# Tiles at new addresses, later rotary angles, and attention latents scaled after their projections

## The chip, the cores and the metric

One NeuronCore of one Trainium2 chip runs the whole program in one launch. The metric is the device time in microseconds (us), as the median of repeated executions; an execution that is profiled also gives a trace with a start and a duration for each instruction.

## The reference, cut to what matters

Two blocks of two layers each work on 256 tokens of width 1024. The first has a gated mixer, a banded attention and two gated feed-forward parts with a short convolution; the second has a hybrid mixer, latent attention (MLA), two feed-forward parts and two gated per-layer embeddings. Everything is float32. The change touches the MLA and the feed-forward part before it:

```python
c = hn @ w_down                       # 384 query latents, 256 key/value latents, 32 rotary
q = (rmsnorm_2(cq, q_norm) @ w_uq).reshape(b, s, MLA_HEADS, MLA_NOPE + MLA_ROPE)
kv = (rmsnorm_2(ckv, kv_norm) @ w_ukv).reshape(b, s, MLA_HEADS, MLA_NOPE + MLA_V)
q = concat([q_nope, apply_rope(q_rope, positions)]); k = concat([k_nope, rope(kr)])
o = causal_softmax_attention(q, k, v, 1 / sqrt(96));  return o.reshape(...) @ w_o
```

`rmsnorm_2` divides each token's row by its root mean square and multiplies by a gain per feature. Both `@` after it are linear, so a token's root may be put on before or after them.

## The kernel before, in words

Activations lie transposed, 128 features in the partitions and 256 tokens along the free axis: `hT` is the residual, `xt` scratch, and `xA`, `xB`, `hid` hold an activation split in a high and a low float32r part. Weights stream from HBM in 203 chunks of 128 x 2048 float32 (1 MB). SyncE loads them into four buffers `raw0..3`, ScalarE rounds each chunk to `w_hi` (`split_hi`, line 504), VectorE makes the rest `w_lo` (`split_lo`, line 1104), and TensorE multiplies: every 128 x 128 block of weights is used in three products, high by high, high by low, low by high.

There are two forms of these products. In the wide form (`three`, lines 1845 to 1847, and `plain`, line 1856, at the start of a stage) the weights are the stationary operand and the activation, 256 tokens of it, is the moving one. In the natural form (`three_natural`, lines 1851 to 1853) it is the other way round: the activation is stationary and 256 (for the MLA's values 512) columns of weights move.

The order is written out by hand on each engine, in program order, with semaphores between engines. `hi_made`, `lo_made` and `chunk_used` count chunks: `split_hi` of a chunk waits until the chunk four before it has been used, and each stage calls the two splits with `.ahead()`, which is three chunks on.

The last feed-forward part before the MLA has 11 chunks in its second half ("down"). When its last gated pair is written (`hid_lo`), GpSimd issues two DMAs, the MLA's constants `ml_con` and the positions `ml_pos` (lines 483, 484). VectorE then waits for both, computes the rotary angles (`rope_angles`, lines 1132 to 1149, ten chained instructions on 128 x 256), and only then starts on the down loop's splits; ScalarE has the sine of the angles (line 613) before its own splits.

In the MLA, `latent` (line 998) copies the down-projection's result to `ml_c`, squares it into `xt`, and rounds the key/value latents into `xA[3:5]`. TensorE sums the squares over the features (`latent_sums`), ScalarE and VectorE make the inverse root (`inverse_root`, `refine`), VectorE scales the latents by gain and root (`scale_latent`), and ScalarE and VectorE split them again (`round_latent`, `rest_latent`). The keys are already computed from latents without their root and scaled when they are read out of PSUM (`k_scale`); the values and the queries use latents with it. Eight products for the keys go to PSUM banks `K_BANK`, the four for the values to `V_BANK`, and the queries' to banks 0 and 1 in turn; a bank's new product waits until its old content has been read out.

Of the kernel before, what the change touches and what calls it, by code (L numbers as in the profile page):

```python
# [27 lines left out]
P = 128  # L28
T = 256
# [60 lines left out]
K_BANK, V_BANK, O_BANK = (0, 1, 2, 3, 7, 0, 1, 2), (3, 7, 0, 1), (0, 1, 6, 7)  # L90
# [37 lines left out]
def build(nc, stream, x_t, vecs, wst, bsp, rel, hyc, w0, lora, mlc, pos, p_t, out):  # L128
    with ExitStack() as ctx:
# [19 lines left out]
        with ExitStack() as ph:  # L149
# [29 lines left out]
            with ExitStack() as f:  # L179
                ml_q = sb("ml_q", [P, KD, T], where=f)  # L180
                ml_rope_q = sb("ml_rope_q", [P, KD, T], where=f)
                ml_k = sb("ml_k", [P, KD, T], where=f)
                ml_v = sb("ml_v", [P, 2, D], where=f)
                ml_c = sb("ml_c", [P, 5, T], where=f)
# [56 lines left out]
        def rows(tile, k, n, part):  # L241

            if isinstance(k, int):
# [251 lines left out]
        def _(act):  # L495
# [62 lines left out]
            def ffn(f, n):  # L558
# [65 lines left out]
            def exponent(a, m):  # L624
                act.wait_ge(max_made, KD * a + m + 1)
                pr, st = probs[a][m % 3], stats[a]
                for i in range(2):
                    for t, (lo, hi) in enumerate(((0, P), (P, 384))):
                        n = 4 * m + 2 * i + t
                        last = nc.scalar.activation(pr[:, i, lo:hi], pr[:, i, lo:hi], ACT.Exp, scale=-1.0,  # L630
                                                    bias=st[:, 0, n:n + 1], accum_out=st[:, 1, n:n + 1])
                last.then_inc(exp_made, 1)
# [376 lines left out]
            def latent_root(j, nth):  # L1009
                act.wait_ge(c_ss, nth)  # L1010
                inverse_root(ml_rs[j], half(4 + j, 0), (384, 256)[j], c_rs)

            def round_latent(k, nth):
                act.wait_ge(c_made, nth)
                nc.scalar.activation(xA[:, k if k < 3 else k + 2, 0, :], xt[:, k, :], ACT.Copy).then_inc(c_hi, 1)

            def v_copy(i):
                wait_up(act, 8 + i)
                t, n = divmod(i, 2)
                nc.scalar.activation(ml_v[:, t, 512 * n:512 * n + 512], ps[:, V_BANK[i], :], ACT.Copy).then_inc(ml_evac, 1)  # L1020
# [12 lines left out]
            latent_root(1, 1)  # L1033
            split_hi(Chunk(c0 + 2).ahead())
            latent(2)
            round_latent(3, 1)
            round_latent(4, 2)
            latent_root(0, 2)
            split_hi(Chunk(c0 + 3).ahead())
            act.wait_ge(fold_done, 1)  # L1040
# [3 lines left out]
            for k in range(3):  # L1044
                round_latent(k, 3 + k)
# [46 lines left out]
        def _(dve):  # L1092
# [104 lines left out]
            def ffn(f, n):  # L1197
# [65 lines left out]
                if f == 2:  # L1263
                    rope_angles()
                with dve.Fori(0, 2) as it:
                    for s in range(RING):
                        split_lo(Chunk(d0 + s, it).ahead())
                if f >= 2:
# [22 lines left out]
            def biased_max(a, m, bias, sign):  # L1291
# [443 lines left out]
            def scale_latent(j, nth):  # L1735

                dve.wait_ge(c_rs, nth)
                refine(ml_rs[j], half(4 + j, 0), (384, 256)[j], ml_pr[1][:, 0, 0:T])
                for k in ((0, 1, 2), (3, 4))[j]:
                    gain = col("q_norm", k) if j == 0 else col("c_norm", k - 3)  # L1740
                    nc.vector.scalar_tensor_tensor(out=xt[:, k, :], in0=ml_c[:, k, :], scalar=gain, in1=ml_rs[j],
                                                   op0=ALU.mult, op1=ALU.mult).then_inc(c_made, 1)

            def rest_latent(k, nth):
                dve.wait_ge(c_hi, nth)
                x = xA[:, k if k < 3 else k + 2]
                nc.vector.tensor_tensor(x[:, 1, :], xt[:, k, :], x[:, 0, :].bitcast(F32), ALU.subtract).then_inc(c_lo, 1)
# [14 lines left out]
            def ml_max(m):  # L1762
                biased_max(1, m, lambda i, t: ml_bias[:, P:T] if t == 0 else ml_bias[:, 0:T], 1.0)
# [10 lines left out]
            nc.vector.tensor_tensor(ml_kr[64:128, :], half(1, 1)[64:128], ml_cs[64:128, :], ALU.mult).then_inc(kr_made, 1)  # L1774
            split_nope_lo(Chunk(c0 + 1).ahead())
            scale_early(N_ML, 2, c0 + 2, 2)
            scale_latent(1, 1)
            k_scale(0)
            k_scale(1)
            rest_latent(3, 1)  # L1780
            rest_latent(4, 2)
            k_scale(2)
            k_scale(3)
# [3 lines left out]
            scale_latent(0, 2)  # L1787
            split_lo(Chunk(c0 + 3).ahead())
            for k in range(3):
                rest_latent(k, 3 + k)  # L1790
# [50 lines left out]
        def _(pe):  # L1841
# [544 lines left out]
            def latent_sums(j, evacs):  # L2386

                ks = ((0, 1, 2), (3, 4))[j]
                pe.wait_ge(c_evac, evacs)
                for k in ks:  # L2390
                    last = plain(half(4 + j, 0), ones, xt[:, k, :], k == ks[0], k == ks[-1])
                last.then_inc(c_ss, 1)
# [25 lines left out]
            pe.wait_ge(c_lo, 2)  # L2418
            for i in range(4):
                t, n = divmod(i, 2)  # L2420
                pe.wait_ge(k_evac, 4 + i)
                for k in range(2):
                    last = three_natural(ps[:, V_BANK[i], :], xA[:, 5 + k, 0, P * t:P * t + P], xA[:, 5 + k, 1, P * t:P * t + P],
# [3 lines left out]
            def q_pair(m):  # L2427

                if m < 2:
                    pe.wait_ge(ml_evac, 3 + m)  # L2430
# [3 lines left out]
                for i in range(6 * m, 6 * m + 6):  # L2434
# [3 lines left out]
                    if i < 3:  # L2438
                        pe.wait_ge(c_lo, 3 + k)
# [233 lines left out]
```

## Time and profile before

| what | us |
|---|---|
| median of 3 runs | 1326.67 (1326.57 to 1328.77) |
| profiled execution | 1328.3 |
| its span, first to last instruction | 1326.5 |
| TensorE busy in the span | 1301.6 |
| VectorE, ScalarE busy | 914.5, 756.9 |
| mean granted TensorE clock | 0.994 of full speed |

A timeline row gives start, duration, engine, line, operation, output and inputs, shape, how many instructions the row merges, and in brackets how long the engine was idle before it and whose work ended that. A matmul's duration overlaps the next one's, since matmuls are pipelined; how fast they go is read from the distance of their starts.

### The profile page before, as it was taken

What the parts mean: (1) busy time and instruction counts of PE and PEld (TensorE: products, weight loads), DVE (VectorE), ACT (ScalarE), POOL (GpSimd) and SP (SyncE); (2) the same over time, 40 slices, a digit from 0 to 9 for tenths busy, and PEclk for the clock granted to TensorE, in tenths of its full rate; (3) what the DMA queues carried; (4) which work ended last, traced back from release to release, by engine and by line L of the source; (5) the groups of instructions that cost most, each with busy time, mean ns of one, the idle gap of its engine ahead of it and who ended that gap; (6) DMA issues with size and microseconds to landing.
All of it is one profiled execution on the core that took longest, in us unless ns stands there. A gap on an engine that the chain in (4) does not pass through costs nothing.

```text
span 1326.5 us, 29295 instructions
## 1 busy us (share of the span) xinstructions
PE 1301.6 (98%) x12212; PEld 1269.2 (96%) x12212; DVE 914.5 (69%) x1296; ACT 756.9 (57%) x981; POOL 44.1 (3%) x37
## 2 busy tenths in 40 slices
PE   9999999999999999999999999999999999999997
PEld 8999999998999999999989899999999889999997
DVE  4779776488479876468746377666488879666556
ACT  6657665367657665357554266554376776554444
POOL 1010000010010000010000010000001001000000
PEclk9999999999999999999999999999999999999999
DMA  8455554545345555535401136553634335555520
GB/s 332 176 206 191 190 190 190 190 191 193 126 159 191 190 190 190 190 122 191 160 34 45 57 135 223 190 187 133 230 131 183 124 127 207 191 190 190 190 96 32
DMA packets 31980, 220.61 MB, mean 166 GB/s; under 512 B 3712, under 2 KB 3840, under 8 KB 6160
## 3 DMA queue, kind: packets, MB, share of 16 engines
q1 hardware_dynamic: 30672, 213.36, 44.3%
q0 software_dynamic: 784, 4.85, 1.1%
q8 instruction: 72, 1.18, 0.4%
q10 hardware_dynamic: 432, 1.05, 0.2%
q14 instruction: 20, 0.16, 0.0%
HBM read 218.20 MB, written 1.05 MB: 165 GB/s over the span
## 4 chain that ended last, share of the span: by engine, by line
PE 85%; DVE 9%; ACT 4%; issue 1%; DMA 1%; POOL 0%; SPq 0%; DVEq 0%; ACTq 0%; POOLq 0%
PE ps L1845 21%; PE ps L1846 21%; PE ps L1847 21%; PE ps L1856 17%; DVE w_lo L1104 3%; PE ps L1851 2%; PE ps L1852 1%; PE ps L1853 1%; ACT w_hi L504 1%; DVE xt L1156 1%; PE ps L2067 1%; DMA raw<-stream 1%; DVE xA L1166 1%; DVE xB L1166 0%; DVE xB L1128 0%
## 5 line engine op out<-in xcount | busy, mean ns | idle before, releaser
L1104 DVE TENSOR_TENSOR w_lo<-raw,w_hi 128x2048 fp32r<-128x2048 f32 x197 | 449.5, 2287 | 147.1 <-ACT w_hi L504 146.7
L504 ACT ACTIVATE w_hi<-raw 128x2048 fp32r<-128x2048 f32 x197 | 375.9, 1913 | 171.1 <-PE ps L1847 165.1
L1845 PE MATMUL ps<-xB,w_hi 128*128 128x256 f32 x1120 | 314.3, 281 | 1.7 <-DVE up_acc L1230 1.7
L1846 PE MATMUL ps<-xB,w_hi 128*128 128x256 f32 x1120 | 312.8, 279 | 0.0
L1847 PE MATMUL ps<-xB,w_lo 128*128 128x256 f32 x1120 | 312.7, 279 | 0.0
L1845 PEld LDWEIGHTS ps<-xB,w_hi 128*128 128x128 f32 x1120 | 210.5, 188 | 3.2 <-DVE up_acc L1230 1.9
L1845 PE MATMUL ps<-xA,w_hi 128*128 128x256 f32 x744 | 211.0, 284 | 1.6 <-ACT ml_v L1020 1.1
L1846 PEld LDWEIGHTS ps<-xB,w_hi 128*128 128x128 f32 x1120 | 210.5, 188 | 0.1
L1847 PEld LDWEIGHTS ps<-xB,w_lo 128*128 128x128 f32 x1120 | 210.5, 188 | 0.0
L1846 PE MATMUL ps<-xA,w_hi 128*128 128x256 f32 x744 | 207.7, 279 | 0.0
L1847 PE MATMUL ps<-xA,w_lo 128*128 128x256 f32 x744 | 207.6, 279 | 0.0
L1845 PE MATMUL ps<-hid,w_hi 128*128 (+1 forms) x704 | 196.6, 279 | 1.8 <-DVE w_lo L1104 1.8
L1846 PE MATMUL ps<-hid,w_hi 128*128 (+1 forms) x704 | 196.5, 279 | 0.0
L1847 PE MATMUL ps<-hid,w_lo 128*128 (+1 forms) x704 | 196.5, 279 | 0.0
L1845 PEld LDWEIGHTS ps<-xA,w_hi 128*128 128x128 f32 x744 | 139.8, 188 | 5.4 <-issue 3.3
L1846 PEld LDWEIGHTS ps<-xA,w_hi 128*128 128x128 f32 x744 | 139.9, 188 | 0.2
L1847 PEld LDWEIGHTS ps<-xA,w_lo 128*128 128x128 f32 x744 | 139.8, 188 | 0.0
L1845 PEld LDWEIGHTS ps<-hid,w_hi 128*128 128x128 f32 x704 | 132.3, 188 | 2.0 <-issue 2.0
L1847 PEld LDWEIGHTS ps<-hid,w_lo 128*128 128x128 f32 x704 | 132.3, 188 | 0.0
L1846 PEld LDWEIGHTS ps<-hid,w_hi 128*128 128x128 f32 x704 | 132.3, 188 | 0.0
L566 ACT ACTIVATE gate_acc<-ps,vec 128x256 f32<-128x256 f32 x88 | 44.8, 560 | 81.1 <-PE ps L1847 81.1
L1856 PE MATMUL ps<-xA,w_hi 128*128 128x256 f32 x480 | 81.1, 285 | 2.6 <-DVE w_lo L1322 1.8
(287 smaller groups left out, 1869.3 us busy)
## 6 DMA issues: line engine op xcount, KB each, us to landing
raw<-stream SPq DMA_DIRECT2D x199, 1024.0 KB, 4.8
raw<-stream SPq DMA_DIRECT2D x4, 512.0 KB, 7.8
at_bias<-rel POOLq DMA_DIRECT2D x1, 2048.0 KB, 8.3
hT<-x_t SPq DMA_DIRECT2D x4, 256.0 KB, 7.0
lora_w<-lora POOLq DMA_DIRECT2D x1, 1024.0 KB, 5.1
out_t<-xt SPq DMA_DIRECT2D x4, 256.0 KB, 2.4
hcon<-hyc POOLq DMA_DIRECT2D x1, 576.0 KB, 4.1
wsT<-wst ACTq DMA_DIRECT2D x1, 512.0 KB, 4.3
```

The lines of the kernel that those rows point to most:

```text
L504: nc.scalar.activation(w_hi[c.slot][:], raw[c.slot][:], ACT.Copy).then_inc(hi_made, 1)
L566: last = nc.scalar.activation(acc[:, b, :], half(bank, b), ACT.Identity, bias=dcol(f"cb{f}", j, off), scale=dcol(f"cw{f}", j, off + 2 * (g ...
L1104: nc.vector.tensor_tensor(w_lo[c.slot][:], raw[c.slot][:], w_hi[c.slot][:].bitcast(F32), ALU.subtract).then_inc(lo_made, 1)
L1156: nc.vector.scalar_tensor_tensor(out=xt[:, k, :], in0=hT[:, k, :], scalar=col(gain, k), in1=rs[:], op0=ALU.mult, op1=ALU.mult).then_inc(xt ...
L1166: last = nc.vector.scalar_tensor_tensor(out=early_tile(n)[:, k, 1, :], in0=hT[:, k, :], scalar=col(EARLY[n][0], k), in1=early_tile(n)[:, k ...
L1845: nc.tensor.matmul(out, wh, xh, start=start, stop=False, skip_group_check=True)
L1846: nc.tensor.matmul(out, wh, xl, start=False, stop=False, skip_group_check=True)
L1847: return nc.tensor.matmul(out, wl, xh, start=False, stop=stop, skip_group_check=True)
L1851: nc.tensor.matmul(out, xh, wh, start=start, stop=False, skip_group_check=True)
L1852: nc.tensor.matmul(out, xh, wl, start=False, stop=False, skip_group_check=True)
L1853: return nc.tensor.matmul(out, xl, wh, start=False, stop=stop, skip_group_check=True)
L1856: return nc.tensor.matmul(out, lhsT, rhs, start=start, stop=stop, skip_group_check=True)
```

## The change

It has three parts. First, tiles are placed anew. The vectors `vec` move from behind the residual to between `raw` and `w_hi`, eight columns wider, and an unused tile of 54 columns goes between `w_lo` and `hT`. As sums of sizes, vectors and spare tile are 2856 + 216 = 3072 bytes, three times 1024. The program's own allocation starts at byte 16512 of a partition and rounds every tile up to 32 bytes, which gives these addresses (the remainders are those of division by 1024 and by 64):

| tile | before | rest of 1024, of 64 | after | rest of 1024, of 64 |
|---|---|---|---|---|
| raw0 | 16512 | 128, 0 | 16512 | 128, 0 |
| w_hi0 | 49280 | 128, 0 | 52160 | 960, 0 |
| w_lo0 | 82048 | 128, 0 | 84928 | 960, 0 |
| hT | 114816 | 128, 0 | 117920 | 160, 32 |
| vec | 123008 | 128, 0 | 49280 | 128, 0 |
| eye_ones | 125856 | 928, 32 | 126112 | 160, 32 |
| xB | 127904 | 928, 32 | 128160 | 160, 32 |
| xt | 144288 | 928, 32 | 144544 | 160, 32 |
| xA | 152480 | 928, 32 | 152736 | 160, 32 |
| hid and the other tiles of a stage | 168864 | 928, 32 | 169120 | 160, 32 |

Second, the angles and their sine move behind the eight splits of the down loop on VectorE and ScalarE.

Third, the query and value latents no longer get their root. The latents are multiplied by their gain alone and split straight out of PSUM; the roots, one number per token, are made in `ml_tok`, with tokens in the partitions. The values take theirs as the scale of `v_copy`, and the queries theirs in the softmax: the row maximum is multiplied by it (one more VectorE instruction for each pair of heads, on 128 x 4) and the exponential gets it as its scale. `K_BANK` and `V_BANK` change, and so do the waits of `q_pair`.

```diff
-K_BANK, V_BANK, O_BANK = (0, 1, 2, 3, 7, 0, 1, 2), (3, 7, 0, 1), (0, 1, 6, 7)
+K_BANK, V_BANK, O_BANK = (3, 7, 0, 1, 2, 3, 7, 0), (1, 2, 3, 7), (0, 1, 6, 7)
         raw = [sb(f"raw{i}", [P, CHUNK]) for i in range(RING)]
+        vec = sb("vec", [P, NV + 8])
         w_hi = [sb(f"w_hi{i}", [P, CHUNK], F32R) for i in range(RING)]
         w_lo = [sb(f"w_lo{i}", [P, CHUNK], F32R) for i in range(RING)]
+        sb("spare", [P, 54])
         hT = sb("hT", [P, KD, T])
-        vec = sb("vec", [P, NV])
...
+                with act.Fori(0, 2) as it:
+                    for s in range(RING):
+                        split_hi(Chunk(d0 + s, it).ahead())
                 if f == 2:
                     act.wait_ge(cs_arg, 1)
                     nc.scalar.activation(ml_cs[:], ml_ang, ACT.Sin).then_inc(cs_made, 1)
-                with act.Fori(0, 2) as it:
-                    for s in range(RING):
-                        split_hi(Chunk(d0 + s, it).ahead())
...
-                nc.scalar.activation(ml_c[:, b:b + n, :], two, ACT.Copy)
                 nc.scalar.activation(xt[:, b:b + n, :], two, ACT.Square).then_inc(c_evac, 1)
+                for k, h in ((((2, 0),), (), ((0, 0), (1, 1)))[s]):
+                    nc.scalar.activation(xA[:, k, 0, :], half(s, h), ACT.Copy, scale=col("q_norm", k)).then_inc(lq_hi, 1)
...
+            def latent_roots():
+                act.wait_ge(c_ss, 2)
+                own.mark(nc.scalar.activation(ml_tok[:, 0:2], ps[:, 4, 0:2], ACT.Ln, bias=col("eps"), scale=1.0 / 384))
+                own.mark(nc.scalar.activation(ml_tok[:, 2:4], ps[:, 4, 2:4], ACT.Copy))
+                own.wait()
+                nc.scalar.activation(ml_tok[:, 0:2], ml_tok[:, 0:2], ACT.Exp, scale=-0.5).then_inc(c_rs, 1)
...
+                if by is not None:
+                    link(last)
+                    mx = st[:, 0, 4 * m:4 * m + 4].rearrange("p (i t) -> p i t", t=2)
+                    last = nc.vector.scalar_tensor_tensor(out=mx, in0=mx, scalar=-1.0,
+                                                          in1=by.unsqueeze(1).broadcast_to([P, 2, 2]), op0=ALU.mult,
+                                                          op1=ALU.mult)
...
+            def rest_query(nth, k, s, h):
+                dve.wait_ge(lq_hi, nth)
+                nc.vector.scalar_tensor_tensor(out=xA[:, k, 1, :], in0=half(s, h), scalar=col("q_norm", k),
+                                               in1=xA[:, k, 0, :].bitcast(F32), op0=ALU.mult,
+                                               op1=ALU.subtract).then_inc(lq_lo, 1)
...
+            def token_sums():
+                pe.wait_ge(k_evac, 1)
+                for t in range(2):
+                    plain(ps[:, 4, 2 + t:3 + t], ml_rs[1][:, P * t:P * t + P], eye[:, 0:1], t == 0, True)
+                for t in range(2):
+                    for k in range(3):
+                        last = plain(ps[:, 4, t:t + 1], xt[:, k, P * t:P * t + P], ones[:, 0:1], False, k == 2)
+                last.then_inc(c_ss, 1)
...
                 elif m == 2:
-                    pe.wait_ge(c_evac, 3)
+                    pe.wait_ge(lq_lo, 1)
                     plain(half(6, 0), ml_fold[64:128, :], ml_kr[64:128, :]).then_inc(fold_done, 1)
+                elif m == 4:
+                    pe.wait_ge(lq_lo, 3)
...
                 if m == 5:
-                    latent_sums(0, 3)
+                    pe.wait_ge(c_evac, 3)
+                    token_sums()
...
-            pe.wait_ge(c_lo, 2)
...
             def q_pair(m):
-                if m < 2:
-                    pe.wait_ge(ml_evac, 3 + m)
+                if m == 0:
+                    pe.wait_ge(k_evac, KD)
+                elif m == 1:
+                    pe.wait_ge(ml_evac, 1)
```

VectorE at the start of the down half, before: after the last pair (`hid`) come the angles (`ml_rs` holds them, `ml_pos` the positions), then the loop with the splits.

```order
L1234 TENSOR_TENSOR hid<-up_acc,hid 128x2x256
L1140 CAST ml_rs<-ml_pos 128x256
L1141 TENSOR_SCALAR ml_rs<-ml_rs,vec 128x256
L1142 TENSOR_SCALAR ml_rs<-ml_rs,vec 128x256
L1143 TENSOR_SCALAR ml_rs<-ml_rs 128x256
L1144 TENSOR_SCALAR ml_rs<-ml_rs 128x256
L1146 SCALAR_TENSOR_TENSOR ml_rs<-ml_rs 128x256 x3
L1147 TENSOR_SCALAR ml_rs<-ml_rs,vec 128x256
L1149 TENSOR_SCALAR ml_rs<-ml_rs 128x256
L1265 UNCONDITIONAL_BRANCH
L1265 ISA
L1104 TENSOR_TENSOR w_lo<-raw,w_hi 128x2048
```

VectorE there after the change: the end of the loop (its branch), the angles, and what follows them.

```order
L1103 TENSOR_TENSOR w_lo<-raw,w_hi 128x2048
L1262 REGISTER_ALU
L1262 COMPARE_AND_BRANCH
L1139 CAST ml_rs<-ml_pos 128x256
L1140 TENSOR_SCALAR ml_rs<-ml_rs,vec 128x256
L1141 TENSOR_SCALAR ml_rs<-ml_rs,vec 128x256
L1142 TENSOR_SCALAR ml_rs<-ml_rs 128x256
L1143 TENSOR_SCALAR ml_rs<-ml_rs 128x256
L1145 SCALAR_TENSOR_TENSOR ml_rs<-ml_rs 128x256 x3
L1146 TENSOR_SCALAR ml_rs<-ml_rs,vec 128x256
L1148 TENSOR_SCALAR ml_rs<-ml_rs 128x256
L1269 TENSOR_TENSOR pl_x<-pl_in,pl_x 128x2x256
```

The ten angle instructions now stand behind eight splits and ahead of the split of the embedding's input (`pl_x`) and the last splits.

VectorE in the MLA before, from the end of the key root's refinement: scaled latents (`xt<-ml_c`), keys (`ml_k`), the latents' low parts (`xA`), weight splits, and the refinement of the query root.

```order
L1123 TENSOR_TENSOR ml_rs<-ml_rs,ml_pr 128x256
L1741 SCALAR_TENSOR_TENSOR xt<-ml_c,vec,ml_rs 128x256 x2
L1751 TENSOR_TENSOR ml_k<-ps,ml_rs 128x256 x2
L1747 TENSOR_TENSOR xA<-xt,xA 128x256 x2
L1751 TENSOR_TENSOR ml_k<-ps,ml_rs 128x256 x2
L1104 TENSOR_TENSOR w_lo<-raw,w_hi 128x2048
L1751 TENSOR_TENSOR ml_k<-ps,ml_rs 128x256 x4
L1120 TENSOR_TENSOR ml_pr<-ml_rs 128x256
L1121 SCALAR_TENSOR_TENSOR ml_pr<-ps,ml_pr 128x256
L1122 TENSOR_SCALAR ml_pr<-ml_pr 128x256
L1123 TENSOR_TENSOR ml_rs<-ml_rs,ml_pr 128x256
L1741 SCALAR_TENSOR_TENSOR xt<-ml_c,vec,ml_rs 128x256 x3
```

The same stretch after the change, as far as the queries' rotary part.

```order
L1122 TENSOR_TENSOR ml_rs<-ml_rs,ml_pr 128x256
L1743 SCALAR_TENSOR_TENSOR xA<-ps,vec,xA 128x256 x2
L1759 TENSOR_TENSOR ml_k<-ps,ml_rs 128x256 x4
L1103 TENSOR_TENSOR w_lo<-raw,w_hi 128x2048
L1759 TENSOR_TENSOR ml_k<-ps,ml_rs 128x256 x4
L1103 TENSOR_TENSOR w_lo<-raw,w_hi 128x2048
L1751 TENSOR_TENSOR ml_tok<-ml_tok 128x2
L1752 SCALAR_TENSOR_TENSOR ml_tok<-ps,ml_tok 128x2
L1754 TENSOR_SCALAR ml_tok<-ml_tok 128x2
L1755 TENSOR_TENSOR ml_tok<-ml_tok 128x2
L1103 TENSOR_TENSOR w_lo<-raw,w_hi 128x2048
L1765 SCALAR_TENSOR_TENSOR ml_rope_q<-ps,ml_cs 64x256 x4
```

The scaled latents and their low parts are gone, two query latents' low parts stand ahead of the keys (the third comes earlier), and the query root's refinement works on 128 x 2.

## Rows read from the trace of the kernel before

**Rows 1.** The page's busy times, and what TensorE waited for.
```profile
PE 1301.6 (98%) x12212; PEld 1269.2 (96%) x12212; DVE 914.5 (69%) x1296; ACT 756.9 (57%) x981; POOL 44.1 (3%) x37
...
PE ps L1845 <- DVE w_lo L1104: 2.3, 2, 1.8
...
PE ps L1845 <- ACT ml_v L1020: 1.1, 1, 1.1
```

**Rows 2.** TensorE's groups: line, tiles, shapes, count, busy us, mean ns.
```profile
L1845 PE MATMUL ps<-xB,w_hi 128*128 128x256 f32 x1120 | 314.3, 281 | 1.7 <-DVE up_acc L1230 1.7
...
L1845 PE MATMUL ps<-xA,w_hi 128*128 128x256 f32 x744 | 211.0, 284 | 1.6 <-ACT ml_v L1020 1.1
L1845 PE MATMUL ps<-hid,w_hi 128*128 (+1 forms) x704 | 196.6, 279 | 1.8 <-DVE w_lo L1104 1.8
...
L1856 PE MATMUL ps<-xA,w_hi 128*128 128x256 f32 x480 | 81.1, 285 | 2.6 <-DVE w_lo L1322 1.8
...
L1851 PE MATMUL ps<-w_hi,xA 128*128 128x256 f32 x96 | 27.6, 287 | 0.0
```

**Rows 3.** TensorE by windows: stretch, us, busy us, matmuls begun or under way.
```profile
26.50:44.00 17.50, 17.50 (x150) 1.00 0.78 298
100.00:150.00 50.00, 50.00 (x431) 1.00 0.53 190
```

**Rows 4.** VectorE's groups with 2048 and with 512 elements.
```profile
L1104 DVE TENSOR_TENSOR w_lo<-raw,w_hi 128x2048 fp32r<-128x2048 f32 x197 | 449.5, 2287 | 147.1 <-ACT w_hi L504 146.7
...
L1234 DVE TENSOR_TENSOR hid<-up_acc,hid 128x512 f32 (+1 forms) x44 | 30.0, 682 | 2.8 <-ACT hid L578 2.8
```

**Rows 5.** Timeline where the down half begins: TensorE, VectorE, ScalarE and GpSimd.
```profile
920.34 0.28 PE L1847 MATMUL ps<-hid,w_lo 128*128 x1
922.45 0.38 PE L1845 MATMUL ps<-hid,w_hi 128*128 x1 [1.83 <-DVE w_lo L1104]
...
913.79 0.30 DVE L1140 CAST ml_rs<-ml_pos 128x256 f32<-128x256 int32 x1 [4.08 <-DMA ml_pos<-pos]
...
917.32 0.29 DVE L1149 TENSOR_SCALAR ml_rs<-ml_rs 128x256 f32<-128x256 f32 x1
...
917.97 7.31 ACT L504 ACTIVATE w_hi<-raw 128x2048 fp32r<-128x2048 f32 x4
...
910.53 0.54 POOL L484 DMA_DIRECT2D ml_pos<-pos  x1
```

**Rows 6.** Timeline of the down half's end: a ScalarE split, VectorE's.
```profile
939.57 1.92 ACT L504 ACTIVATE w_hi<-raw 128x2048 fp32r<-128x2048 f32 x1 [3.68 <-PE ps L1847]
...
941.52 2.29 DVE L1104 TENSOR_TENSOR w_lo<-raw,w_hi 128x2048 fp32r<-128x2048 f32 x1 [3.31 <-ACT w_hi L504]
...
909.00 1.28 ACT L613 ACT_TABLE_LOAD   x1
```

**Rows 7.** Timeline of the MLA's keys, values and first queries.
```profile
1018.10 0.27 PE L1847 MATMUL ps<-xA,w_lo 128*128 128x256 f32 x1
1018.89 0.70 PE L1856 MATMUL ps<-ml_kr,ml_con 64*128 64x256 f32 x2 [0.51 <-ACT xt L1004]
...
1021.75 1.46 PE L1856 MATMUL ps<-xt,eye_ones 128*128 128x256 f32 x6
1022.86 0.47 PE L1845 MATMUL ps<-xA,w_hi 128*128 128x256 f32 x1
...
1030.54 0.40 PE L1853 MATMUL ps<-w_hi,xA 128*128 128x512 f32 x1
1032.03 0.39 PE L1845 MATMUL ps<-xA,w_hi 128*128 128x256 f32 x1 [1.09 <-ACT ml_v L1020]
...
1018.86 0.43 DVE L1123 TENSOR_TENSOR ml_rs<-ml_rs,ml_pr 128x256 f32<-128x256 f32 x1
```

**Rows 8.** Groups of small instructions: one moving column, and 128 x 4 on VectorE.
```profile
L1856 PE MATMUL ps<-eye_ones,xt 128*128 128x1 f32 x8 | 0.9, 240 | 0.0
...
L1307 DVE RECIPROCAL ml_st<-ml_st 128x4 f32<-128x4 f32 x8 | 1.4, 173 | 1.1 <-ACT ml_pr L630 1.1
```

More of the change, by code:

```diff
@@ L183, in build @@
                 ml_v = sb("ml_v", [P, 2, D], where=f)
-                ml_c = sb("ml_c", [P, 5, T], where=f)
+                ml_tok = sb("ml_tok", [P, 5 * T], where=f)
                 ml_pr = [sb(f"ml_pr{i}", [P, 2, 384], where=f) for i in range(3)]
@@ L629, in exponent @@
                         n = 4 * m + 2 * i + t
-                        last = nc.scalar.activation(pr[:, i, lo:hi], pr[:, i, lo:hi], ACT.Exp, scale=-1.0,
-                                                    bias=st[:, 0, n:n + 1], accum_out=st[:, 1, n:n + 1])
+                        last = nc.scalar.activation(pr[:, i, lo:hi], pr[:, i, lo:hi], ACT.Exp,
+                                                    scale=ml_tok[:, t:t + 1] if a else -1.0, bias=st[:, 0, n:n + 1], accum_out=st[:, 1, n:n + 1])
                 last.then_inc(exp_made, 1)
@@ L1019, in v_copy @@
                 t, n = divmod(i, 2)
-                nc.scalar.activation(ml_v[:, t, 512 * n:512 * n + 512], ps[:, V_BANK[i], :], ACT.Copy).then_inc(ml_evac, 1)
+                nc.scalar.activation(ml_v[:, t, 512 * n:512 * n + 512], ps[:, V_BANK[i], :], ACT.Copy,
+                                     scale=ml_tok[:, 2 + t:3 + t]).then_inc(ml_evac, 1)
             def q_copy(m):
@@ L1032, in _ @@
             split_nope_hi(Chunk(c0 + 1).ahead())
-            latent_root(1, 1)
+            act.wait_ge(c_ss, 1)
+            inverse_root(ml_rs[1], half(5, 0), 256, c_rs)
             split_hi(Chunk(c0 + 2).ahead())
             latent(2)
-            round_latent(3, 1)
-            round_latent(4, 2)
-            latent_root(0, 2)
             split_hi(Chunk(c0 + 3).ahead())
+            latent_roots()
             act.wait_ge(fold_done, 1)
@@ L1043, in _ @@
             v_copy(1)
-            for k in range(3):
-                round_latent(k, 3 + k)
             split_hi(Chunk(c0 + 4).ahead())
@@ L1288, in ffn, with biased_max @@
                     split_lo(Chunk(C0["at_k"]).ahead())
-            def biased_max(a, m, bias, sign):
+            def biased_max(a, m, bias, sign, by=None):
                 dve.wait_ge(scored, KD * a + m + 1)
@@ L1733, in split_nope_lo, with query_root @@
                                         ALU.subtract).then_inc(lo_made, 1)
[L1735 to L1747, printed above, removed]
+            def rest_query(nth, k, s, h):
[3 more added lines that the diff above has]
+                                               op1=ALU.subtract).then_inc(lq_lo, 1)
+            def query_root():
+                dve.wait_ge(c_rs, 2)
+                y, tmp = ml_tok[:, 0:2], ml_tok[:, 4:6]
+                link(nc.vector.tensor_tensor(tmp, y, y, ALU.mult))
+                link(nc.vector.scalar_tensor_tensor(out=tmp, in0=ps[:, 4, 0:2], scalar=EPS * 384, in1=tmp, op0=ALU.add,
+                                                    op1=ALU.mult))
+                link(nc.vector.tensor_scalar(tmp, tmp, 0.5 / 384, -1.5, ALU.mult, ALU.add))
+                link(nc.vector.tensor_tensor(y, y, tmp, ALU.mult))
             def k_scale(m):
@@ L1762, in ml_max @@
             def ml_max(m):
-                biased_max(1, m, lambda i, t: ml_bias[:, P:T] if t == 0 else ml_bias[:, 0:T], 1.0)
+                biased_max(1, m, lambda i, t: ml_bias[:, P:T] if t == 0 else ml_bias[:, 0:T], 1.0, ml_tok[:, 0:2])
             split_nope_lo(Chunk(c0).ahead())
@@ L1774, in _ @@
             nc.vector.tensor_tensor(ml_kr[64:128, :], half(1, 1)[64:128], ml_cs[64:128, :], ALU.mult).then_inc(kr_made, 1)
+            rest_query(1, 2, 0, 0)
             split_nope_lo(Chunk(c0 + 1).ahead())
             scale_early(N_ML, 2, c0 + 2, 2)
[L1777 to L1783, printed above, removed]
+            dve.wait_ge(c_rs, 1)
+            refine(ml_rs[1], half(5, 0), 256, ml_pr[1][:, 0, 0:T])
+            rest_query(3, 0, 2, 0)
+            rest_query(3, 1, 2, 1)
+            for m in range(4):
+                k_scale(m)
             split_lo(Chunk(c0 + 2).ahead())
@@ L1786, in _ @@
                 k_scale(m)
-            scale_latent(0, 2)
             split_lo(Chunk(c0 + 3).ahead())
-            for k in range(3):
-                rest_latent(k, 3 + k)
+            query_root()
             split_lo(Chunk(c0 + 4).ahead())
@@ L2384, in _, with latent_sums @@
             ple(0)
[L2386 to L2391, printed above, removed]
+            def latent_sums():
+                pe.wait_ge(c_evac, 2)
+                plain(half(5, 0), ones, xt[:, 3, :], True, False)
+                plain(half(5, 0), ones, xt[:, 4, :], False, True).then_inc(c_ss, 1)
+            def token_sums():
[5 more added lines that the diff above has]
+                        last = plain(ps[:, 4, t:t + 1], xt[:, k, P * t:P * t + P], ones[:, 0:1], False, k == 2)
                 last.then_inc(c_ss, 1)
@@ L2422, in _ @@
                 for k in range(2):
-                    last = three_natural(ps[:, V_BANK[i], :], xA[:, 5 + k, 0, P * t:P * t + P], xA[:, 5 + k, 1, P * t:P * t + P],
+                    last = three_natural(ps[:, V_BANK[i], :], xA[:, 3 + k, 0, P * t:P * t + P], xA[:, 3 + k, 1, P * t:P * t + P],
                                          *weight(c, KD * k + 4 * n, 4), k == 0, k == 1)
```

19 lines of the change are left out of this document (5 added, 14 removed).

## The prediction

> **What bounds the kernel now.** I read the page's busy times first, then TensorE's list of waits, then its groups, and the timeline only where a wait stands. TensorE is busy for 1301.6 of 1326.5 us, and the waits that touch this change are short: 2.3 us on the weights' low parts in two pieces, 1.1 us on the values' copies [rows 1]. So the time is the number of matmuls times their distance, plus a few gaps. VectorE at 69% and ScalarE at 57% are covered nearly everywhere.
>
> The distance of starts is not the 0.28 us that a row gives as duration. In a stretch of wide products, 431 matmuls are begun or under way in 50 us; without the two already running at its left edge that is 50 / 429 = 0.1166 us each. In a stretch of natural products it is 17.5 / 148 = 0.1182 us [rows 3]. Each natural matmul costs 1.6 ns more at the same shape and full clock, and between the two forms the tiles change roles. This is the one place in the trace where an effect of placement on TensorE may show, so it prices the first part.
>
> **Part 1, tiles placed anew.** No instruction is added or moved by it, so it can only act through the distance of matmuls and the durations of the other engines. The wide form has 3 x (1120 + 744 + 704) = 7704 matmuls, and line 1856 has four groups of split weights with 1248 more, of which the first has 480 [rows 2]: some 8950. The natural form at 256 columns has 480 (three lines, 96 with `xA` as in the row shown and 64 with `xB`) [rows 2]. One nanosecond in the wide form is 9 us of the kernel. The bounds come from the only difference that rows show, 1.6 ns: 8950 x 1.6 = 14.3 us up or down, less or more 0.8 us for the natural form.
>
> Which value? If the difference comes from where a stationary row starts within 64 bytes (weights at a rest of 0, activations at 32), nothing changes, since these rests are the same after: w stays at 0, x at 32, and only `hT` goes from 0 to 32. If it comes from the distance of moving and stationary tile modulo 1024, the two forms swap: x minus w is 928 - 128 = 800 before and 160 - 960 = -800 after. I take the first, zero, because the finer rest is the simpler cause of a fixed cost per load, and because the form itself (which operand is the activation) may be the cause, which no address changes. VectorE gives no sign of a cost of placement: from 512 elements at 682 ns in tiles at a rest of 928 to 2048 at 2287 ns in tiles at 128 it is 1605 ns for 1536 elements [rows 4], one straight line through two placements. Even 0.1 us more for each of its 197 splits would lie in its idle time.
>
> The Trainium skill ("TensorE: Matmul & The Clock Gate", section "Wait — 56ns, not 53.3ns?") states a distance of N / 2.4 GHz plus 2.5 ns at full clock, 109.2 ns for 256 columns. The trace disagrees by 7.4 ns on every float32r matmul; by that rule, if placement were what stands between, 8950 of them would give back 66 us. No row here shows 109 ns for these products in any placement, so I give this 2 in 100.
>
> **Part 2, the angles later.** VectorE waits for the positions' DMA, issued at 910.53, until 913.79; its ten instructions end at 917.61 [rows 5]. ScalarE's first split of the down half begins only at 917.97, after the sine, four then run in a row, and TensorE, which had used up the chunks made ahead, stands from 920.34 to 922.45: 2.11 us from start to start instead of 0.12, and 0.11 us more for a slower first pair. The gain is 2.1 us if the angles cost nothing in their new place.
>
> Do they? In the loop ScalarE starts on a chunk when TensorE frees its buffers, at 939.57, and VectorE has it done at 943.81, 4.24 us later [rows 6]. TensorE needs it three chunks of 48 x 0.1166 = 5.6 us after 939.57, that is 16.8: slack 12.6 us. In the new order the eighth low part is followed by the angles (3.8 us), then on ScalarE the sine with its table load (1.28 + 0.4) and the embedding's input (0.6). The ninth split, due 5.6 us after the eighth, starts 4.2 + 3.8 + 1.7 + 0.6 = 10.3 us after it: 4.7 us late of 12.6. The tenth is 1 us late, the eleventh on time, before VectorE adds the first quarter to the residual. DMAs keep their order; the load behind the late split is needed four chunks on. Cover: VectorE's idle 3.31 us per chunk [rows 6]. If it failed, the 2.1 us would only move.
>
> **Part 3, latents without roots.** Taken off: three copies to `ml_c`, five scalings, five roundings and rests of latents, one refinement on 256 columns. What was on TensorE's path:
> - The fold of the rotary key waited for the squares of the last latents (0.79 us from 1018.10 to 1018.89 [rows 7]). Now it waits for a low part that VectorE makes before the second nope split. Gain 0.67 us.
> - Queries waited until the values were copied: 1.49 us from the last value product at 1030.54 to 1032.03 [rows 7], where 0.23 are its own length. They now need the keys read out and, for the second pair, one value copy. Gain 1.26 us.
> - The sums of squares: six matmuls of 256 columns take 1.11 us (1021.75 to 1022.86 [rows 7]). The new ones are 8 calls of one column, 16 matmuls; eight such have 0.9 us of busy time together [rows 8], so 1.8 us, bounded by 16 x 0.24 = 3.8 above. Loss 0.7 us (to 2.7).
>
> Late next is the first use of the query latents. The key root is refined by 1019.29 [rows 7]; two low parts of 0.48 behind it end at 1020.2. The fifth key product, which overwrites their bank, is due at 1020.1 to 1020.2: a tie, at most 0.5 us. The weights' low parts for the queries come earlier than before. In the softmax, eight times one VectorE instruction like the 128 x 4 one at 0.17 us [rows 8], with a semaphore step 0.25, lengthens the chain from scores to exponential; two products of queries (2.1 us) stand between. Price nothing, bound 8 x 0.25 = 2 us. Part 3 in sum: 0.67 + 1.26 - 0.7 = 1.2 us gained.
>
> **Sum.** 0 + 2.1 + 1.2 = 3.3 us off. Against the profiled execution that is 1328.3 - 3.3 = 1325.0, its span 1323.2; the profiled execution lies 1.6 us above the median of the runs, so the median goes from 1326.67 to 1323.4. A change below 0.2% (2.65 us) counts as none.
>
> **Rivals.**
> - *Roles swapped.* The wide products go to 0.1182 us, by the mirrored distance of 800 and -800. For it: the two rates are in the trace, and nothing else differs in shape or clock. Against it: the 64-byte rests stay, and the form is a sufficient cause. 1323.4 + 14.3 - 0.8 = 1337: slower. It decides from 0.37 ns a matmul (3.3 / 8950) on.
> - *Placement relieves a collision.* All tiles that meet in a matmul lay 224 bytes from one another's rest before, as now, but with different absolute rests, and `raw` no longer shares one with `w_hi`. If wide products lose 1.6 ns, 1323.4 - 14.3 - 0.8 = 1308; half of it gives 1316. For it: 0.1166 us is not an obvious floor, 256 columns at 2.4 GHz being 0.1067. Against it: no row shows these products faster in any placement.
> - *The saved waits come back.* The sums take 3.8 us, the fifth key product waits 0.5 us, the maxima 1 us: 1323.4 + 2.0 + 0.5 + 1.0 = 1326.9, no change. For it: three edges with little slack within 20 us. Against it: each wait is behind work that rows show done.
>
> **How the numbers follow.** Forecast (placement neutral, both waits gone) 45 in 100; roles swapped 20; relief 20, and 2 more for the large one; waits come back 13. The forecast's own range is 1321 to 1326. Relief reaches to 1308 and the swap to 1337, so the range is 1307.5 to 1337.5. Of the forecast's 45 some 7 land above -2.65 us, as does most of the last rival. Faster: 38 + 21 + 1 = 60; within 0.2%: 7 + 1 + 11 = 19; slower: 20 + 1 = 21.
>
> **What would show it.** In a window of the up half, 429 starts in 50 us if placement is neutral, 423 if roles swap, 435 with relief; in the gated mixer the natural products' 148 would move the other way. TensorE has no wait on `w_lo` in the down half, and the eleven chunks take 61.6 us on end. ScalarE's ninth split is some 5 us late with TensorE unmoved. Queries start 0.23 us after the last value product, and the one-column matmuls take 1.8 us. A wide distance that moves by more than 0.4 ns would make the forecast wrong, as would a gap at the fifth key product of over 1 us.

## The result: slower by 8 us, and the profile after

The changed kernel takes 1335.11 us (1333.84 to 1335.63, 4 runs) against 1327.16 for the kernel before, timed beside it: a ratio of 1.0057, 95% interval 1.0044 to 1.007, so 5.8 to 9.3 us slower. I had forecast 3.3 us faster. The time lies inside the range, the direction is wrong, and the rival called "roles swapped" describes what happened.

The page of the changed kernel has 10.5 us more of busy TensorE than [rows 1] at almost the same count of matmuls. The waits on the weights' low parts in the down half and on the values' copies, both in [rows 1], are gone; what is left of waits on `w_lo` are pieces of 0.4 to 0.8 us, the two largest at the start of the program.

```profile
span 1333.0 us, 29315 instructions
...
PE 1312.1 (98%) x12222; PEld 1280.0 (96%) x12222; DVE 913.2 (69%) x1297; ACT 758.4 (57%) x977; POOL 44.1 (3%) x37
...
PE ps L1862 <- ACT slot L902: 2.3, 4, 1.0
PE ps L1862 <- DVE xB L1127: 2.0, 1, 2.0
PE ps L1851 <- DVE up_acc L1229: 1.4, 1, 1.4
...
PE ps L1862 <- DVE w_lo L1327: 0.8, 1, 0.8
```

The windows of TensorE answer to [rows 3]: stretch, us, busy us, matmuls begun or under way, granted clock, share of the DMA engines and GB/s.

```profile
26.50:44.00 17.50, 17.50 (x152) 1.00 0.78 300
100.00:150.00 50.00, 50.00 (x425) 1.00 0.54 190
1110.00:1160.00 50.00, 50.00 (x425) 1.00 0.56 193
```

Without the two that are under way at the left edge, the natural products come every 17.5 / 150 = 0.1167 us (0.1182 before) and the wide ones every 50 / 423 = 0.1182 us (0.1166 before). The two forms have changed places to within 0.1 ns, at full clock in both kernels. Further down I give these distances in ns, as the mean from start to start inside a chunk: 118.3 ns for wide products now, 116.7 before. The duration that a row shows hides it: it is 282 ns where [rows 2] had 281. A matmul reaches over the next two starts, and its duration is no measure of their distance.

```profile
L1103 DVE TENSOR_TENSOR w_lo<-raw,w_hi 128x2048 fp32r<-128x2048 f32 x197 | 449.9, 2288 | 154.4 <-ACT w_hi L504 154.1
...
L1851 PE MATMUL ps<-xB,w_hi 128*128 128x256 f32 x1120 | 316.4, 282 | 1.4 <-DVE up_acc L1229 1.4
```

VectorE's split, for [rows 4], is unchanged at 2288 ns (2287 before), and ScalarE's rounding of a chunk takes 1918 ns where it took 1913. Neither engine bounds the time, so what counts is the distance of TensorE's matmuls.

### The profile page after: what moved, and what is told of

It reads as the page before. It is cut to its first block, busy times and chain, and to the rows that moved or that the text cites. A ratio compares the mean times of both kernels' runs of the same rounds, so it can differ in the third digit from the quotient of the medians.

```text
span 1333.0 us, 29315 instructions
## 1 busy us (share of the span) xinstructions
PE 1312.1 (98%) x12222; PEld 1280.0 (96%) x12222; DVE 913.2 (69%) x1297; ACT 758.4 (57%) x977; POOL 44.1 (3%) x37
## 4 chain that ended last, share of the span: by engine, by line
PE 91%; DVE 5%; ACT 2%; issue 1%; DMA 1%; SPq 0%; DVEq 0%; ACTq 0%
PE ps L1851 22%; PE ps L1852 22%; PE ps L1853 22%; PE ps L1862 19%; PE ps L1857 2%; PE ps L1858 2%; PE ps L1859 2%; DVE w_lo L1103 1%; PE ps L2073 1%; ACT w_hi L504 1%; DMA raw<-stream 1%; DVE xt L1155 1%; DVE xB L1165 0%; ACT slot L902 0%; DVE xB L1127 0%
## 5 line engine op out<-in xcount | busy, mean ns | idle before, releaser
L1103 DVE TENSOR_TENSOR w_lo<-raw,w_hi 128x2048 fp32r<-128x2048 f32 x197 | 449.9, 2288 | 154.4 <-ACT w_hi L504 154.1
L504 ACT ACTIVATE w_hi<-raw 128x2048 fp32r<-128x2048 f32 x197 | 377.1, 1918 | 174.9 <-PE ps L1853 170.5
L1851 PE MATMUL ps<-xA,w_hi 128*128 128x256 f32 x744 | 212.1, 285 | 0.0
L1852 PE MATMUL ps<-xA,w_hi 128*128 128x256 f32 x744 | 209.0, 281 | 0.0
L1207 DVE SCALAR_TENSOR_TENSOR gate_acc<-ps,vec,gate_acc 128x254 f32<-128x254 f32 x88 | 38.3, 477 | 68.3 <-ACT gate_acc L566 68.3
```

The costliest lines, as they stand in the source:

```text
L504: nc.scalar.activation(w_hi[c.slot][:], raw[c.slot][:], ACT.Copy).then_inc(hi_made, 1)
L1103: nc.vector.tensor_tensor(w_lo[c.slot][:], raw[c.slot][:], w_hi[c.slot][:].bitcast(F32), ALU.subtract).then_inc(lo_made, 1)
L1207: nc.vector.scalar_tensor_tensor(out=acc[:, b, 2:T], in0=half(bank, b)[:, 0:T - 2], scalar=dcol(f"cw{f}", j, off), in1=acc[:, b, 2:T], op0 ...
L1851: nc.tensor.matmul(out, wh, xh, start=start, stop=False, skip_group_check=True)
L1852: nc.tensor.matmul(out, wh, xl, start=False, stop=False, skip_group_check=True)
```

## The experiments

Theory A: the placement alone slows the wide products, and the two other parts gain what I forecast. Theory B: the moved instructions do it. The first four kernels take the change apart; each was timed in 5 rounds.

**Placement alone** (kernel before, tiles of the changed one).

```diff
         raw = [...]
+        vec = sb("vec", [P, NV + 8])
         w_hi, w_lo = ...
+        sb("spare", [P, 54])
         hT = sb("hT", [P, KD, T])
-        vec = sb("vec", [P, NV])
```

> The kernel before with the new placement alone (vec between the raw and the split weights with 8 more columns, 54 columns of spare ahead of hT), no instruction changed. Theory A (placement alone slows the wide products): the wide distance is 118.3 ns instead of 116.7 and the natural one 116.8 instead of 118.3, as in the changed kernel; 8950 x 1.66 = 14.9 us more, less 480 x 1.6 = 0.8, less up to 3 us that two half-clock stretches of the kernel before give back (65.6 to 69.0 and 581.1 to 584.3 us, 213 ns from start to start; the changed kernel has neither): 1327.2 + 11 to 14 = 1338 to 1341 us. Theory B (something in the moved instructions changes the distance, such as what VectorE and ScalarE do beside it): wide distance 116.7, 1327 us.

Measured: 1337.75 us, ratio 1.0082 (1.0069 to 1.0095), so 10.5 us slower with not one instruction changed; wide distance 118.3 ns. Theory B falls. The time is 0.25 us below what was expected; what is known of that stands under "The size" below.

**Later angles and rootless latents alone** (changed kernel, the diff above reversed).

> The changed kernel with the tiles of the kernel before (later angles and rootless latents alone). Theory A: wide distance 116.7 ns, and the gains of parts 2 and 3 stand alone: 2.1 + 1.2 by my prediction, 2.4 + 2.1 by the excess over 117 ns that the two traces show in the down half and in the latents' stretch; 1327.2 - 3.3 to 4.5 = 1322.7 to 1323.9 us, faster than both. Theory B: wide distance 118.3 ns and some 1335 us.

Measured: 1323.29 us, ratio 0.9972 (0.9963 to 0.9981), wide distance 116.7 ns. This beats both kernels. It lies 0.1 us from my forecast of 1323.4 for the whole change, and so close by luck: 4.0 us are gained where 3.3 were priced, and the kernel before stood at 1327.28 beside it and not at 1326.67.

**The angles alone.**

```diff
-                if f == 2:
-                    rope_angles()          # and the sine on ScalarE
                 with dve.Fori(0, 2) as it:
                     ...
+                if f == 2:
+                    rope_angles()
```

> The kernel before with the angles and the sine behind the down half's splits, nothing else. Both theories leave the wide distance at 116.7 ns. If the wait of 2.0 us at the start of the third layer's down half simply goes: 1327.2 - 2.1 = 1325.1 us. If it comes back later (the ninth split of the down half, or the latents' start): 1327 us and a new gap over 1 us between 925 and 1005 us.

Measured: 1325.26 us, ratio 0.9988 (0.998 to 0.9997): 2.0 us faster. Set side by side by equal matmuls, the profile goes from 1.1 us behind the kernel before to 1.0 us ahead across the start of the third down half and stays there to the end; nothing comes back.

**The latents alone** (both parts alone, with the angles put back).

```diff
+                if f == 2:
+                    rope_angles()          # and the sine on ScalarE
                 with dve.Fori(0, 2) as it:
                     ...
-                if f == 2:
-                    rope_angles()
```

> The kernel before with the rootless latents and the banks of keys and values, nothing else. Gaps before the fold and before the queries gone, one-column sums in place of six matmuls: 1.2 us gained by the prediction, 2.1 us by the excess over 117 ns that the two traces show between 1003 and 1110 us: 1325.0 to 1326.0 us. The rival, that the new sums and the longer chain from scores to exponentials cost as much: 1327.2 us and up.

Measured: 1326.45 us, ratio 0.9996 (0.9987 to 1.0004): 0.8 us, not told from nothing by its own timing, and 0.45 us above what was expected. Its trace, like that of the two parts together, gains 1.5 us across the keys, values and first queries, from 1018 to 1083 us of the kernel before.

Placement alone and the two parts together add up: 10.5 - 4.0 = 6.5 us, within the interval of the whole change. The two parts apart give 2.0 + 0.8 = 2.8 of the 4.0, which their intervals allow.

**Two maps.** What in the placement counts? In one kernel the four pairs of split weights can lie at different rests, and `xB` and `xA` (with `hid`, directly behind it) too, so that one trace holds eight pairs of tiles.

```diff
-        w_hi = [...]; w_lo = [...]
+        wa_hi, wa_lo, 64 bytes, wb_hi, wb_lo, 64 bytes, wc_hi, wc_lo, 64 bytes, wd_hi, wd_lo
+        sb("xB_pad", [P, 8])          # second map: [P, 72]
         xB ...
+        sb("xA_pad", [P, 8])
         xA ...
```

(The line of the weights is put in short: each tile is declared in this order, with 64 unused bytes where it says so.)

> A map: rootless latents and later angles on the tiles of before, with the four pairs of split weights (named wa to wd) starting at 128, 192, 256 and 320 modulo 512, xB at 128 and xA with hid at 160. Read: the wide distance for each pair of tiles. Theory D (distance of the moving from the stationary tile, modulo 128, 32 fast and 96 slow): wa,xA and wc,xA 116.7 ns, wb,xA and wd,xA 118.3; with xB all distances are 0 or 64, of which no row says anything yet. Theory S (where the stationary tile starts, modulo 512: 128 and 160 fast, 416 and 448 slow): wa fast with either x, wb to wd the same whichever x they meet. Theory M (where the moving tile starts, modulo 512: 416 and 448 fast, 128 and 160 slow): all eight pairs near 118.3. Time: none is fixed by a theory, 1323 (all fast) to 1337 us (all slow).

> The same map with xB at 384 and xA with hid at 416 modulo 512. wa,xA repeats the pair of the kernel before (128 and 416): 116.7 ns by every theory. Theory D: wa,xA and wc,xA 116.7, wb,xA and wd,xA 118.3. Theory S: each of wa to wd as in the other map. Theory M: all with xA at 116.7.

Measured: 1336.01 and 1337.09 us, one run each (kernel before 1327.47). The timeline of the first map has the first matmul of five chunks in a row of 48 matmuls each, in a down half:

```profile
540.52 0.28 PE L1859 MATMUL ps<-hid,wa_hi 128*128 x1
...
546.12 0.28 PE L1859 MATMUL ps<-hid,wb_hi 128*128 x1
...
551.80 0.29 PE L1859 MATMUL ps<-hid,wc_hi 128*128 x1
...
557.50 0.28 PE L1859 MATMUL ps<-hid,wd_hi 128*128 x1
...
563.26 0.28 PE L1859 MATMUL ps<-hid,wa_hi 128*128 128x256 f32 x1
```

The chunks take 5.60, 5.68, 5.70 and 5.76 us, that is 116.7, 118.3, 118.7 and 120.0 ns a matmul, all with `hid` at 160 and weights at 128, 192, 0 and 64 modulo 256. So the stationary tile's place alone isn't it either: `wa` gives 116.7 ns with `hid` but 119.8 with `xB`. Theories S and M fall, and so does D as put (modulo 128), since `wc` would have been fast. The second map, with all moving tiles 256 bytes further, gives the same rate in each pair, but for one chunk to which I come below. What fits is the distance of moving minus stationary tile modulo 256: 32 before (that is 800), 224 after (that is -800).

**The same distances at other addresses.**

```diff
-        sb("xB_pad", [P, 8]); sb("xA_pad", [P, 8])
+        sb("xB_pad", [P, 32]); sb("xA_pad", [P, 32])
```

> The first two maps agree in every pair although all moving tiles lie 256 bytes further in the second, and give by distance (moving minus stationary tile, modulo 256): 0 119.8 ns, 32 116.8, 64 117.6 to 117.8, 96 120.0 and 119.7, 128 118.6, 160 118.5 (hid) and 118.7 (xA), 192 117.8, 224 118.4. This map has the stationary wa to wd at 128, 192, 0, 64 modulo 256 as there, but xB at 224 and xA with hid at 96. Theory D256 (the distance alone counts, modulo 256): xB with wa 120.0, wb 116.8, wc 118.4, wd 118.5; xA with wa 118.4, wb 118.5, wc 120.0, wd 116.8. Rival P (each pair of rests has its own price, and 32 was fast because one tile stood at 128): wb,xB (192 and 224) and wd,xA (64 and 96) not at 116.8.

Measured: 1337.42 us, one run (kernel before 1328.18). The timeline of an up half, again the first matmuls of five chunks:

```profile
110.45 0.28 PE L1859 MATMUL ps<-xB,wa_hi 128*128 128x256 f32 x1
...
116.21 0.28 PE L1859 MATMUL ps<-xB,wb_hi 128*128 128x256 f32 x1
...
121.82 0.28 PE L1859 MATMUL ps<-xB,wc_hi 128*128 128x256 f32 x1
...
127.50 0.29 PE L1859 MATMUL ps<-xB,wd_hi 128*128 128x256 f32 x1
...
133.20 0.28 PE L1859 MATMUL ps<-xB,wa_hi 128*128 128x256 f32 x1
```

5.76, 5.61, 5.68 and 5.70 us, or 120.0, 116.9, 118.3 and 118.7 ns, for distances 96, 32, 224 and 160: the four values of the first map to 0.2 ns, in the order that D256 gives, with other tiles at other addresses. With `xA` and `hid` 32 gives 116.7 as well. Rival P falls. One cell is not clean: at 160 about a third of this map's chunks run at 120.0 ns instead of 118.7, and in each of the first three maps a few run at 117.3.

**A finer map**, weights at offsets inside their tiles (`xB` at 160, `xA` and `hid` at 192 modulo 256).

```diff
+        wa, wb, wc, wd = (tile)[:, 2 * i:2 * i + CHUNK]   # 0, 8, 16, 24 bytes
```

> A finer map: later angles and rootless latents, split weights wa to wd beginning 0, 8, 16 and 24 bytes behind 128 modulo 256 (inside tiles that overlap by that much), xB at 160 and xA with hid at 192: distances 32, 24, 16, 8 with xB and 64, 56, 48, 40 with xA. If the steps of 32 bytes are the grain: 116.8 with all of xB's or 119.8 for 8 to 24, and 117.7 with all of xA's. If it is finer, a distance between may lie below 116.7, down to 256 / 2.4 = 106.7 by the column count; one that does would be worth 9 us of the kernel a nanosecond.

Measured: 1336.91 us, one run. The first matmuls of five chunks with `xB`, for distances 24, 16, 8 and 32:

```profile
161.88 0.28 PE L1856 MATMUL ps<-xB,wb_hi 128*128 128x256 f32 x1
...
167.79 0.28 PE L1856 MATMUL ps<-xB,wc_hi 128*128 128x256 f32 x1
...
173.42 0.28 PE L1856 MATMUL ps<-xB,wd_hi 128*128 128x256 f32 x1
...
179.07 0.28 PE L1856 MATMUL ps<-xB,wa_hi 128*128 128x256 f32 x1
...
184.73 0.28 PE L1856 MATMUL ps<-xB,wb_hi 128*128 128x256 f32 x1
```

5.91, 5.63, 5.65 and 5.66 us. The grain is finer than 32 bytes. The map also shows the limit of the rule: the pair at 32 bytes runs at 116.7 ns in the first chunks of an up half and at 117.8 in the later ones, though its addresses are the same, and the pair at 24 bytes runs at 117.7 or 123.3.

All four maps together, both forms, by distance in bytes modulo 256: ns from start to start, as the mean of the last 30 intervals of each whole chunk of 48 matmuls at full clock, with the number of chunks.

| distance | most chunks | other chunks |
|---|---|---|
| 0 | 120.0 (32) | |
| 8 | 117.6 (16) | |
| 16 | 117.3 (10) | 120.0 (7) |
| 24 | 123.3 (12) | 117.7 (4) |
| 32 | 116.7 (58) | 117.8 (9) |
| 40 | 120.0 (12) | |
| 48 | 116.7 (12) | |
| 56 | 117.8 (9) | 116.7 (1), 123.3 (1) |
| 64 | 117.8 (42) | |
| 96 | 120.0 (53) | |
| 128 | 118.7 (34) | |
| 160 | 118.7 (36) | 120.0 (9), 117.3 (8) |
| 192 | 117.8 (33) | 113.3 (2) |
| 224 | 118.3 (52) | |

No distance has its usual rate below 116.7 ns, but two chunks at 192 do run below it: one of the natural form in the finer map (`wa` at 128 moves, `xA` at 192 is stationary) and one of the wide form in the second map (`xB` at 384 against `wb` at 192). The rows show the first and the last start of a steady stretch: 42 intervals in 4.76 us, and 36 in 4.08, which is 113.3 ns each, held nearly from the chunk's start to its end.

```profile
35.17 0.28 PE L1864 MATMUL ps<-wa_hi,xA 128*128 128x256 f32 x1
...
39.93 0.28 PE L1864 MATMUL ps<-wa_hi,xA 128*128 128x256 f32 x1
```

```profile
70.93 0.28 PE L1859 MATMUL ps<-xB,wb_hi 128*128 128x256 f32 x1
...
75.01 0.28 PE L1859 MATMUL ps<-xB,wb_hi 128*128 128x256 f32 x1
```

The other 33 chunks at 192 run at 117.8. What set these two apart was not tested. If all 8950 wide products could be held there, 3.3 ns each would be some 30 us (an estimate from these rows).

**Both directions of the proof**: the changed kernel with 64 bytes more, and the kernel before with 64 bytes more.

```diff
-        sb("spare", [P, 54])     # changed kernel
+        sb("spare", [P, 70])
...
+        sb("spare", [P, 16])     # kernel before
         eye_ones = sb("eye_ones", [P, 2 * P])
```

> The changed kernel with 16 columns (64 bytes) more in its spare tile, nothing else: weights stay at 192 modulo 256, activations go from 160 to 224, so the distance is 32 again. Theory D256: wide distance 116.7 ns, natural 118.3, and the time of the version with later angles and rootless latents on the tiles of before, 1323.3 us (1322 to 1325), 11.8 below the changed kernel. Rival P (the rests of before themselves are what is fast, or vec between raw and split weights is what is slow): 118 ns or more, 1335 us or more.

> The kernel before with a spare tile of 16 columns (64 bytes) ahead of eye_ones, nothing else: weights at 128, activations from 160 to 224 modulo 256, distance 96 instead of 32. Theory D256: wide distance 120.0 ns as the maps gave for 96 in hid and xA, so 8950 x 3.3 = 29.5 us more in matmuls; of the 14.1 us that 118.3 ns costs by the same count 12.6 came through between two traces, so 26 to 29 us: 1353 to 1357 us. Rival: a distance that is uniform over all tiles behaves otherwise than in the maps, where neighbouring chunks lie at other distances: anything else than 120.0.

Measured, 5 rounds each: 1323.61 us, ratio 0.9971 (0.9959 to 0.9982), for the first, 1353.31, ratio 1.0197 (1.018 to 1.0215), for the second. The windows of the first, and then of the second:

```profile
100.00:150.00 50.00, 50.00 (x431) 1.00 0.55 190
1110.00:1160.00 50.00, 50.00 (x431) 1.00 0.57 202
```

```profile
100.00:150.00 50.00, 50.00 (x419) 1.00 0.54 190
1110.00:1160.00 50.00, 50.00 (x416) 1.00 0.57 205
```

429 starts again in the first. In the second, 417 in the stretch of wide products alone (50 / 417 = 0.1199 us); its later stretch holds the end of a norm, which the shift in time brought into the window. So kernels in which all weights and activations lie at one distance come out at the rates of the maps: 116.7 ns at 32, 118.3 at 224, 120.0 at 96. Both times are as expected. Sixteen columns of unused memory give the changed kernel 11.5 us back, and cost the kernel before 26.3 us. `vec` between the raw and the split weights is innocent.

## Why the prediction was wrong, step by step

**The step that failed** is the value in part 1: "I take the first, zero, because the finer rest is the simpler cause". [Rows 3] already held the effect. The two rates there were one mechanism seen from both sides, since the natural form swaps the roles of the tiles and so turns a distance of 32 into 224. I had written down that reading (800 and -800) and priced it, and set it below a 64-byte rest for which no row spoke. What it was priced at nothing for costs 10.5 us when it is made alone. The kernel before with 64 bytes more is the test of that reason: all rests modulo 64 stay, and it costs 26.3 us. The other reason, that the form itself sets the rate, falls with the changed kernel, where the natural form is the fast one.

**The size.** Priced were 14.3 - 0.8 = 13.5 us. With equal instructions at either placement (the two parts alone against the changed kernel), matmuls of equal number drift apart by 0.287 us every 20 us wherever TensorE doesn't wait, 172 x 1.67 ns, and by 12.6 us in all. The timing of placement alone gave 10.5. A part of the difference is the clock. In the profile of the kernel before, an idle time of 2.0 us is followed by a stretch at the lower level of 1.2 GHz:

```profile
63.32:65.63 2.31, 0.29 (x4) 1.00 0.42 103
65.99:69.00 3.01, 3.01 (x16) 0.50 0.49 207
```

In the changed kernel the same idle time is there and the clock stays up:

```profile
63.98:66.25 2.27, 0.28 (x3) 1.00 0.59 115
66.25:69.50 3.25, 3.25 (x27) 1.00 0.57 242
```

Such a stretch costs 14 x (213 - 117) = 1.3 us, and the kernel before has another at 581.1 us, behind idle times of 1.3 and 0.7 us (15 intervals of 213 ns, 1.4 us), that the changed one hasn't. With placement alone one stands behind the wait that the later angles remove, the first row below is the wait, and the second what follows 1.1 us behind it:

```profile
924.90:927.04 2.14, 0.28 (x4) 1.00 0.00 0
928.17:931.37 3.20, 3.20 (x17) 0.50 0.90 356
```

Which executions get one is not settled: the kernel before spreads from 1325.1 to 1330.1 us over 29 runs at one chip, mostly the longer the lower its granted clock. What remains of the 13.5 us, about 1 to 2 us, may have gone into waits that slower matmuls shorten; that isn't shown.

**Part 2, the angles: right.** Priced 2.1 us, timed 2.0. In the changed kernel TensorE has no start-to-start gap over 130 ns from 900 to 974 us. The timeline of the down half's end shows the price where it was put: ScalarE, then VectorE.

```profile
949.23 1.92 ACT L504 ACTIVATE w_hi<-raw 128x2048 fp32r<-128x2048 f32 x1 [3.76 <-PE ps L1853]
951.17 1.28 ACT L616 ACT_TABLE_LOAD   x1
957.24 0.42 ACT L616 ACTIVATE ml_cs<-ml_rs 128x256 f32<-128x256 f32 x1 [4.79 <-DVE ml_rs L1148]
957.56 0.61 ACT L619 ACTIVATE pl_x<-pl_in 128x512 fp32r<-128x512 f32 x1
958.08 1.90 ACT L504 ACTIVATE w_hi<-raw 128x2048 fp32r<-128x2048 f32 x1
```

```profile
951.18 2.29 DVE L1103 TENSOR_TENSOR w_lo<-raw,w_hi 128x2048 fp32r<-128x2048 f32 x1 [3.39 <-ACT w_hi L504]
953.39 0.29 DVE L1139 CAST ml_rs<-ml_pos 128x256 f32<-128x256 int32 x1
...
956.91 0.29 DVE L1148 TENSOR_SCALAR ml_rs<-ml_rs 128x256 f32<-128x256 f32 x1
```

The ninth split starts at 958.08, 8.85 us behind the eighth where 5.68 is the pace: 3.2 us late, not 4.7. My sum of 10.3 us had the table load behind the angles; it runs at 951.17 beside the low part and the angles, while ScalarE waits for them.

**Part 3, the latents: right in sum.** Priced 1.2 us, in the traces 1.5 (timed alone 0.8, with an interval of -0.5 to 1.7). Its places, in the changed kernel:

```profile
1022.67 0.28 PE L1853 MATMUL ps<-xA,w_lo 128*128 128x256 f32 x1
1022.88 0.70 PE L1862 MATMUL ps<-ml_kr,ml_con 64*128 64x256 f32 x2
...
1025.74 0.50 PE L1862 MATMUL ps<-eye_ones,ml_rs 128*128 128x1 f32 x4
1026.11 1.48 PE L1862 MATMUL ps<-eye_ones,xt 128*128 128x1 f32 x12
1027.45 0.37 PE L1851 MATMUL ps<-xA,w_hi 128*128 128x256 f32 x1
```

The fold follows 0.21 us behind the key product (0.79 in [rows 7]; gain 0.58 of 0.67). The sums take 1.71 us, from 1025.74 to 1027.45 (priced 1.8, loss 0.6 against [rows 7]); the estimate from eight one-column matmuls in [rows 8] held. Nothing waits at the fifth key product, and the queries start 0.23 us behind the last value product as written (1035.02 to 1035.25), which is 1.26 us. The third pair of scores starts 0.25 us behind the last query product (1047.06 us), the other pairs 0.21 us; whether the longer softmax chain makes this 0.04 us I haven't traced. The saved waits did not come back, so the third rival is out too.

**The rivals.** "Placement relieves a collision" didn't happen here: no distance in the table has a usual rate below 116.7 ns. Its ground, that 116.6 ns is no floor, holds all the same: two chunks at distance 192 ran at 113.3. The 109.2 ns that I had worked out, as an estimate, from the rule of the Trainium skill ("TensorE: Matmul & The Clock Gate", "Wait — 56ns, not 53.3ns?") appear in no chunk.

The page "SBUF — State Buffer" of the Trainium skill, in "A bandwidth-pool intuition that's wrong (but worth ruling out)", gives the weight load a second, independent read port and says that contention is structural, not a matter of sharing. The traces don't fit full independence: usual start-to-start distances from 116.7 to 123.3 ns follow how the two operands' addresses lie to each other. Where in the chip the two meet, and why one pair has two rates, no run here shows.

## What to carry to other kernels

Where TensorE is busy for 98% of the span, count starts in a window before and after any change of allocation, even one of unused bytes: 1.67 ns on 8950 matmuls, 15 us, is more than the two scheduling gains together. If one trace holds two rates for the same shape at the same clock, find what differs between them before pricing the difference at nothing; here one run with 16 columns of spare memory would have told it. And keep the distance of stationary and moving tiles on purpose, in a line of the allocation, as part of the tuning.

## What the runs showed of the hardware that I had not expected

- Split matmuls of 256 columns at full clock have a distance that depends on the moving minus the stationary address modulo 256 bytes, with a sign (32: 116.7 ns, 224: 118.3) and a grain of at most 8 bytes (24: 123.3, 32: 116.7, 40: 120.0). The steady values 116.7, 118.3, 120.0 and 123.3 are 280, 284, 288 and 296 periods of 2.4 GHz.
- The distance doesn't fix the rate alone. The same pair of tiles ran at 116.7 or 117.8 ns (distance 32), 117.7 or 123.3 (24), 117.3 or 120.0 (16), and 117.8 or, in two chunks of 35, 113.3 (192; 272 periods). That what ran before a chunk decides it is likely and not shown.
- VectorE's split of 2048 elements took 2287 or 2288 ns in every placement of the whole kernel. ScalarE's rounding took 1912 to 1913 ns with the weights at 128 modulo 256 and 1917 to 1918 with them at 192: 0.3%, hidden here behind TensorE.
- Idle times of TensorE of 0.7 to 2.0 us sometimes bring some 3 us at 1.2 GHz behind them and sometimes not, in the same place with the same instructions.
